# State space of a hybrid block: the row of steps and the chain of decays move into the convolution's stage, ScalarE makes the decays, and the sums over stretches keep the constant stationary

## The reference, cut to what matters

```python
def ssd_chunked(x, dt, A, B, C):
    b, L = x.shape[0], x.shape[1]
    nc = L // CHUNK
    G, K, P, N = N_SSM_GROUPS, HEADS_PER_GROUP, SSM_HEAD_DIM, D_STATE
    xdt = (x * dt[..., None]).reshape(b, nc, CHUNK, G, K, P)
    dA = (dt * A).reshape(b, nc, CHUNK, G, K).transpose(0, 1, 3, 4, 2)
    Bc = B.reshape(b, nc, CHUNK, G, N)
    Cc = C.reshape(b, nc, CHUNK, G, N)
    A_cum = jnp.cumsum(dA, axis=-1)
    Lmat = segsum_exp(dA)
    CB = jnp.einsum("bclgn,bcsgn->bcgls", Cc, Bc)
    y_diag = jnp.einsum("bcgls,bcgkls,bcsgkp->bclgkp", CB, Lmat, xdt)
    decay_states = jnp.exp(A_cum[..., -1:] - A_cum)
    states = jnp.einsum("bclgn,bcgkl,bclgkp->bcgkpn", Bc, decay_states, xdt)
    chunk_decay = jnp.exp(A_cum[..., -1])
    ...   # prev: the states of all chunks before, h = chunk_decay * h + states
    prev = jnp.moveaxis(prev, 0, 1)
    y_off = jnp.einsum("bclgn,bcgkpn,bcgkl->bclgkp", Cc, prev, jnp.exp(A_cum))
    return (y_diag + y_off).reshape(b, L, G, K, P)

def ssd_branch(z, xbc, dt_raw, conv_w, conv_b, dt_bias, a_log, d_skip, norm_w):
    b, L = z.shape[0], z.shape[1]
    xbc = jax.nn.silu(causal_depthwise_conv(xbc, conv_w, conv_b))
    ...
    xh = xs.astype(jnp.float32).reshape(b, L, N_SSM_GROUPS, HEADS_PER_GROUP, SSM_HEAD_DIM)
    dt = jax.nn.softplus(dt_raw.astype(jnp.float32) + dt_bias.astype(jnp.float32))
    dt = dt.reshape(b, L, N_SSM_GROUPS, HEADS_PER_GROUP)
    A = -jnp.exp(a_log.astype(jnp.float32)).reshape(N_SSM_GROUPS, HEADS_PER_GROUP)
    y = ssd_chunked(xh, dt, A, Bs.astype(jnp.float32), Cs.astype(jnp.float32))
    y = y + d_skip.astype(jnp.float32).reshape(N_SSM_GROUPS, HEADS_PER_GROUP)[..., None] * xh
    ...
```

## Time and profile before

| | us |
|---|---|
| median of 3 timed runs | 3831.87 (3828.68 to 3834.31) |
| the profiled execution | 3840.37, its span 3839.1 |
| mean granted clock of TensorE | 0.974 |
| PE busy | 3601.2, 94% of the span |
| DVE busy | 2043.1, 53% |
| ACT busy | 1398.2, 36% |
| POOL busy | 388.6, 10% |
| convolution's stage | from 660 to 820 |
| chain of steps | from 820 to 834 |
| state space | from 834 to 941 |

### The profile page before, as it was taken

How to read it: one execution, slowest core, us unless ns; L and a number is a source line. 1 busy time by engine, 2 the same in 40 slices (tenths; PEclk the granted TensorE clock), 3 DMA queues, 4 the chain that set the end, 5 groups by cost and what they waited for, 6 DMA issues and landing times. The chain is left out here.

```text
span 3839.1 us, 44288 instructions
## 1 busy us (share of the span) xinstructions
PE 3601.2 (94%) x17148; PEld 2924.7 (76%) x17148; DVE 2043.1 (53%) x3283; ACT 1398.2 (36%) x2423; POOL 388.6 (10%) x362
## 2 busy tenths in 40 slices
PE   8999999988998999989999989998999998989999
PEld 7877877876776887767887778877776777767777
DVE  4546465769536424741344466666466475562256
ACT  2224343321523223536223353354343232343244
POOL 1000000036001100013010100000000123121100
PEclk9999999989999999999999999999999999999999
DMA  6445311210223323520322232254201220132355
GB/s 235 176 173 179 116 39 61 88 40 28 84 92 115 124 94 127 171 71 6 105 81 75 93 99 94 94 174 142 82 23 48 72 77 12 39 111 88 93 178 162
DMA packets 106126, 380.16 MB, mean 99 GB/s; under 512 B 11760, under 2 KB 14592, under 8 KB 105792
## 3 DMA queue, kind: packets, MB, share of 16 engines
q1 hardware_dynamic: 100944, 364.86, 29.1%
q0 software_dynamic: 2896, 10.38, 0.9%
q10 hardware_dynamic: 2080, 2.10, 0.2%
HBM read 375.19 MB, written 2.10 MB: 98 GB/s over the span
## 5 line engine op out<-in xcount | busy, mean ns | idle before, releaser
L396 DVE TENSOR_TENSOR w_low<-ring,w_high 128x1024 fp32r<-128x1024 f32 (+1 forms) x637 | 811.9, 1275 | 1019.9 <-ACT w_high L384 1012.5
L420 PE MATMUL bank<-x_low,w_high 128*128 128x512 f32 (+1 forms) x2560 | 1000.2, 394 | 58.3 <-DVE w_low L396 15.8
L384 ACT ACTIVATE w_high<-ring 128x1024 fp32r<-128x1024 f32 (+1 forms) x637 | 670.6, 1053 | 897.1 <-PE bank L420 375.7
L420 PE MATMUL bank<-x_high,w_low 128*128 128x512 f32 (+1 forms) x2560 | 989.2, 390 | 0.0
L420 PE MATMUL bank<-x_high,w_high 128*128 128x512 f32 (+1 forms) x2560 | 636.0, 387 | 0.0
L420 PEld LDWEIGHTS bank<-x_low,w_high 128*128 128x128 f32 x2560 | 495.4, 194 | 162.1 <-issue 23.8
L420 PEld LDWEIGHTS bank<-x_high,w_low 128*128 128x128 f32 x2560 | 496.0, 194 | 97.0 <-issue 1.4
L420 PEld LDWEIGHTS bank<-x_high,w_high 128*128 128x128 f32 x2560 | 467.1, 192 | 99.2 <-issue 1.9
L482 PE MATMUL bank<-w_low,x_high 128*128 128x512 f32 (+3 forms) x416 | 156.9, 377 | 1.4 <-ACT z_z L1665 1.3
L484 PE MATMUL bank<-w_high,x_high 128*128 128x512 f32 (+3 forms) x416 | 155.7, 374 | 0.0
L483 PE MATMUL bank<-w_high,x_low 128*128 128x512 f32 (+3 forms) x416 | 155.5, 374 | 0.0
(11 more groups left out here) (624 smaller groups left out, 5738.2 us busy)
## 6 DMA issues: line engine op xcount, KB each, us to landing
ring<-in_W SPq DMA_DIRECT2D x688, 512.0 KB, 3.5
f_hid<-in_xT ACTq DMA_DIRECT2D x2, 1024.0 KB, 11.6
X<-in_x POOLq DMA_DIRECT2D x1, 2048.0 KB, 11.8
out<-X SPq DMA_DIRECT2D x4, 512.0 KB, 3.8
const<-in_consts POOLq DMA_DIRECT2D x1, 1389.0 KB, 6.1
f_norm<-in_ln_g POOLq DMA_DIRECT2D x2, 512.0 KB, 8.9
f_norm<-in_ln_b POOLq DMA_DIRECT2D x2, 512.0 KB, 10.6
ring<-in_W SPq DMA_DIRECT2D x2, 432.0 KB, 3.1
```

Of the source, the lines that this page charges most:

```text
L384: ac.activation(b.UH[i % NU][:, 0:src.shape[1]], src, ACT.Copy).then_inc(*b.split.act.up("high", i))
L396: dv.tensor_tensor(b.UL[i % NU][:, 0:n], src, b.UH[i % NU][:, 0:n].bitcast(F32), SUB).then_inc(*b.split.dve.up("low", i))
L420: i = pe.matmul(out, w[:, k, c], v, start=n == 0 and q == 0, stop=last and q == 3 * K - 1)
```

## The change

- dt1's unit comes before x1's in the list, and its matmuls, splits and additions before the convolution's tiles.
- The convolution's tiles run in the order 16 to 23, then 0 to 15 (`ORDER1`); the buffers go by position n instead of by m.
- The chain runs inside the convolution: ScalarE's part behind the copy of n=1, VectorE's behind n=3, PE's behind n=5, the exp into E3 behind the copy of n=7.
- LH is made by ScalarE, 8 activations (Copy with a pointer scale) of 128x128 per unit, two units ahead, instead of by POOL; it is now `incl` * DA.
- seg has the constant `after` as its stationary operand and LH as the moving one, 512 columns in one matmul, instead of LH stationary and `incl` moving, 128 columns in each of four.
- ScalarE no longer waits for the convolution's seal; LH, EE, CB and the softplus buffers lie apart from the convolution's buffers. PE waits for the last silu ahead of each bc.

```diff
@@ Mix1.__init__
+        self.LH = [a.take("s1_lh", 8, 128) for _ in range(2)]
+        sp = Area(b, a.at)
+        self.sp = [sp.take("s1_tmp", 4, 32) for _ in range(3)]
+        self.EE = [a.take("s1_ee", 8, 128) for _ in range(2)]
+        self.CB = [a.take("s1_cb", 128) for _ in range(2)]
         at = a.at
         self.cb = [a.take("c1_in", 516) for _ in range(3)]
...
@@ mix1_units
-    for m in range(24):
+    rows_units(b, s.gcv, "dt1", "w_in", [(ODT, 32)])
+    for m in ORDER1:
         b.unit(("x1", m), "w_in", down_rows(8), [(OX + 128 * m, 128)], lambda m=m: s.gcv.pe.at("x1", m))
-    rows_units(b, s.gcv, "dt1", "w_in", [(ODT, 32)])
...
+ORDER1 = list(range(16, 24)) + list(range(16))
+def tensor_steps(b, s):
     ...   # the three products of DA, out of tensor_ssd1
...
@@ tensor_conv1
+    tensor_rows(b, g, "dt1", b.x, lambda t: b.bank(("dt1", t), g.dve.at("dt", t)))
+    for n, m in enumerate(ORDER1):
...
+        turn(n - 1)
+        if n == 5:
+            tensor_steps(b, s)
+    turn(23)
...
@@ scalar_conv1
+    scalar_rows_ahead(b, "dt1")
+    for n, m in enumerate(ORDER1):
...
+        if n == 1:
+            ac.wait_ge(*g.dve.at("dt", 3))
+            scalar_softplus(b, s.gd.act, "dt", s.DT, s.sp[0])
+            ac.wait_ge(*b.arrived("a_log"))
+            ac.activation(s.al, s.al, ACT.Exp).then_inc(*s.gd.act.up("a"))
+        if n == 7:
+            ac.wait_ge(*s.gd.pe.at("e3"))
+            ac.activation(s.E3, b.bk["e3"][:, 0:384].rearrange("p (c q h) -> p c q h", c=4, q=3),
+                          ACT.Exp).then_inc(*s.gd.act.up("e3"))
...
+        if n >= 11:
+            ac.wait_ge(*g.pe.at("turned", ORDER1[n - 3]))
...
@@ vector_conv1 (its dt additions first)
+        turn(n - 1)
+        if n == 3:
+            vector_steps(b, s)
...
@@ tensor_ssd1
+            pe.wait_ge(*s.gcv.act.at("silu", 23))
             pe.matmul(bank.ap[:, 0:128], s.BT[:, q, sl], s.CT[:, q, sl], start=True,
                       stop=True).then_inc(*g.pe.up("bc", i))
-            pe.wait_ge(*g.pool.at("lh", i))
+            pe.wait_ge(*g.act.at("lh", i))
             for h in range(2):
...
-                for k in range(4):
-                    x = pe.matmul(bank.ap[:, k * 128:(k + 1) * 128], s.LH[i % 2][:, 4 * h + k, :], incl,
-                                  start=True, stop=True)
-                x.then_inc(*g.pe.up("seg", i, h))
+                pe.matmul(bank.ap, b.const("after"), s.LH[i % 2][:, 4 * h:4 * h + 4, :], start=True,
+                          stop=True).then_inc(*g.pe.up("seg", i, h))
...
@@ scalar_ssd1
+    def decays(i):
+        if i >= 16:
+            return
+        c, q = s.ssd[i]
+        if i >= 2:
+            ac.wait_ge(*g.pe.at("seg", i - 2, 1))
+        for k in range(8):
+            h = q * 8 + k
+            x = ac.activation(s.LH[i % 2][:, k, :], b.const("incl"), ACT.Copy, scale=s.DA[:, c, h:h + 1])
+            x.then_inc(*(f.up("lh", i) if k == 7 else f.up()))
+
+    for i in range(2):
+        decays(i)
     for i in range(16):
...
+        decays(i + 2)
...
@@ gpsimd_ssd1
-    gp.wait_ge(*g.dve.at("da"))
     gp.wait_ge(*g.act.at("e3"))
...
-        if i >= 2:
-            gp.wait_ge(*g.pe.at("seg", i - 2, 1))
-        gp.tensor_tensor(s.LH[i % 2], bc(b.const("after"), 1, 8), bc(s.DA[:, c, q * 8:q * 8 + 8], 2, 128),
-                         MUL).then_inc(*f.up("lh", i))
...
@@ scalar_program
     scalar_conv1(b, m1)
     b.seal("conv1", "act")
-    for w in b.sealed("conv1"):
-        ac.wait_ge(*w)
     scalar_ssd1(b, m1)
```

More of the change, by code:

```diff
@@ L1130, in __init__ @@
         a = Area(b, at)
[L1131 to L1135, removed]
         self.XD = [a.take("s1_xd", 512) for _ in range(3)]
@@ L1376, in scalar_att1 @@
             ac.activation(es, es, ACT.Exp).then_inc(*f.up("exp", i))
[L1382 to L1405, removed]
@@ L1408, in scalar_conv1 @@
[L1408 to L1421, removed]
@@ L1424, in vector_conv1 @@
[L1424 to L1440, removed]
-        dv.tensor_scalar(y, x[:, 0:512], b.col("conv_w", m), b.col("conv_b", m), MUL, ADD).then_inc(*f.up())
-        for j in range(1, 4):
-            dv.wait_ge(*f.now())
-            dv.scalar_tensor_tensor(y, x[:, j:j + 512], b.col("conv_w", 24 * j + m), y, MUL,
-                                    ADD).then_inc(*(f.up("conv", m) if j == 3 else f.up()))
[L1446 to L1453, removed]
@@ L1456, in gpsimd_conv1 @@
-def gpsimd_conv1(b, s):
-    for i in range(3):
-        b.nc.gpsimd.memset(s.cb[i][:, 0:3], 0.0).then_inc(*s.gcv.pool.up("zero", i))
-def tensor_ssd1(b, s):
+ORDER1 = list(range(16, 24)) + list(range(16))
+def tensor_steps(b, s):
     pe, g = b.nc.tensor, s.gd
-    incl, units, N = b.const("incl"), s.ssd, 16
     bank = b.bank("e3", g.act.at("e3"))
@@ new lines, in vector_steps, with vector_conv1, turn @@
+def vector_steps(b, s):
+    dv, g, f = b.nc.vector, s.gd, s.gd.dve
+    vector_softplus(b, f, g, "dt", s.DT, *s.sp)
+    dv.wait_ge(*f.now())
+    dv.wait_ge(*g.act.at("a"))
+    dv.scalar_tensor_tensor(s.DA, s.DT, -1.0, bc(s.al, 1, 4), MUL, MUL).then_inc(*f.up("da"))
+def vector_conv1(b, s):
+    dv, g, f = b.nc.vector, s.gcv, s.gcv.dve
+    vector_rows_ahead(b, "dt1")
+    dv.wait_ge(*b.arrived("dt_bias"))
+    for t in range(4):
+        dv.wait_ge(*g.pe.at("dt1", t))
+        dv.tensor_tensor(s.DT[:, t, :], b.bk["dt1", t][:, 0:32], s.dtb, ADD).then_inc(*f.up("dt", t))
+    def turn(n):
+        if n < 0 or ORDER1[n] >= 20:
+            return
+        m = ORDER1[n]
+        dst = s.BM[:, :, m - 16, :] if m >= 16 else s.XS[:, :, m * 128:(m + 1) * 128]
+        dv.wait_ge(*g.pe.at("turned", m))
+        dv.tensor_copy(dst, b.bk["xt1", m].rearrange("p (t c) -> p t c", t=4)).then_inc(*f.up("turned", m))
+    dv.wait_ge(*g.pool.at("zero", 2))
+    for n, m in enumerate(ORDER1):
+        vector_ahead(b, ("x1", m))
+        x, y = s.cb[n % 3], s.cy[n % 3]
+        dv.wait_ge(*g.act.at("copied", m))
+        if n >= 3:
+            dv.wait_ge(*g.act.at("silu", ORDER1[n - 3]))
+        dv.tensor_scalar(y, x[:, 0:512], b.col("conv_w", m), b.col("conv_b", m), MUL, ADD).then_inc(*f.up())
+        for j in range(1, 4):
+            dv.wait_ge(*f.now())
+            dv.scalar_tensor_tensor(y, x[:, j:j + 512], b.col("conv_w", 24 * j + m), y, MUL,
+                                    ADD).then_inc(*(f.up("conv", m) if j == 3 else f.up()))
+        turn(n - 1)
+        if n == 3:
+            vector_steps(b, s)
+    turn(23)
@@ L1476, in tensor_ssd1, with gpsimd_conv1 @@
+def gpsimd_conv1(b, s):
+    for i in range(3):
+        b.nc.gpsimd.memset(s.cb[i][:, 0:3], 0.0).then_inc(*s.gcv.pool.up("zero", i))
+def tensor_ssd1(b, s):
+    pe, g = b.nc.tensor, s.gd
+    units, N = s.ssd, 16
     for r in range(N + 4):
@@ L1544, in vector_ssd1 @@
     units, N = s.ssd, 16
[L1545 to L1548, removed]
     dv.wait_ge(*g.act.at("e3"))
```

35 lines of the change are left out of this document (28 added, 7 removed).

## The result

The changed kernel takes 3807.3 us (median of four runs, 3799.5 to 3813.3), the kernel before 3830.4 in the runs beside it: ratio 0.9937, 95% interval 0.9916 to 0.9958, so 24 us less, 16 to 32. A second comparison gave 0.9934 (0.9913 to 0.9954).

A forecast was written before the change was run, and what follows sets the result against it. TensorE was taken to bound the convolution, latency the chain, VectorE the state space. Terms 2.0 - 0.4 + 2.6 + 13.7 + 82.1 + 1.0 = 101.0 us against 120.8, so -19.8: median 3812.1 us, range 3806.5 to 3824.5.

The forecast's parts named there:

- B: State space rounds: VectorE's long instructions are not GpSimd's doing, rounds stay at 7.1 us; gain 5.9 us, chance 0.09.
- C: State space: ScalarE loads tables in every unit, 6.0 us per round instead of 5.6; gain 15 us, chance 0.04.
- D: Pipeline fill and state space: the clock stays at the half level, slower than before, say 3840 us; chance 0.05.
- A: State space: GpSimd's skip holds VectorE up elsewhere, +1.0 us in 12 rounds; gain 7.8 us, chance 0.12.
- step 7: State space rounds: VectorE 5.60 us and TensorE 5.62, level; y(0) to z1 82.1 us plus 1.0 for stalls.
- step 5: Convolution's tail, no longer covered by dt1: y(0) 13.7 us after the last tile's end, bounds 11.6 and 16.
- Steps 1 to 3: Up to the convolution's end: dt1 ahead of x1 +2.0 us, tile order -0.4, chain moved into the convolution +2.6.
- Step 6: seg in the state space: two matmuls of 512 columns replace eight of 128, 1.72 us instead of 2.12.

The follow-up runs named there:

- the GpSimd run: The changed kernel with the decays made by GpSimd again, in one instruction per unit; ratio 0.9985 to the kernel before.
- the run with eight matmuls: The changed kernel with seg in eight matmuls of 128 columns again, decays still by ScalarE; ratio 0.9932 to the kernel before.
- the second execution: The changed kernel run again with no edit; ratio 0.9934 to the kernel before.
- the move alone: The kernel before with only dt1 in front, BT and CT first and the chain in the convolution; decays by GpSimd, seg in eight matmuls; ratio 0.9983.

## Why the mechanism was right and the sum too small

The mechanisms held; the size did not. Most of my signs were there: the sum at 0.68 in ten of twelve rounds, TensorE's idle time in the rounds gone, no idle TensorE around tiles 4 to 7, L1394 inside the convolution without a wait, one table load behind the last silu, the rounds nearly level between VectorE (77.3 us) and TensorE (79.45). Three had other sizes: rounds of 5.45 us instead of 5.6 to 5.7, decays of 2.44 instead of 2.2, y(0) after 12.5 us instead of 14. B fell (the GpSimd run), C fell (one load, 3.3 us a unit), D fell (half clock only until 835.5). A came up in the first two rounds with yo, and in three of the run with eight matmuls, and cost nothing.

The sum was -19.8 and the stretch says -24.2 (z1's shift -24.0). What failed is the price of TensorE's round in step 7, and with it a smaller part of step 5. By the steps:

- *Steps 1 to 3, up to the last tile's end:* I had it move by 16.3 + 2.0 - 0.4 + 2.6 = 20.5; it moved from 803.67 to 824.78, 21.1. The half clock behind dt1 cost 2.5 (677 to 682), in the bounds of 0 to 5; L1394 cost 2.60. 0.6 too little. The chain under cover cost nothing, as I had it.
- *Step 5, the fill:* 13.7 forecast, 12.5 measured. The mis-sized part is the clock: I had the full level back 8.1 us behind the silu, in the middle of seg(1), counted from seg(0) on, though the last turn and bc(0) stand ahead of it (829.33). It was back at 835.5 (6.2 us behind the silu), with seg(1) just begun (835.56), so bc(1) took 0.42 instead of 0.7 and seg(1) 1.72 instead of 2.5. In the second execution it came back within seg(1), which took 1.99.
- *Step 7, the rounds, is the term that carried most of the miss:* 83.1 forecast, 79.45 measured. bc was taken at 0.39 from the earlier trace rows; in the changed kernel it is 0.22: 14 x 0.17 = 2.4. The 1.0 for stalls did not come up, though VectorE was only 2 us from full. These two are 3.4 of the 3.65.
- *Step 6:* seg's new form at 1.72 was right (1.73), so the sum is not touched, but the credit was wrong. The old form costs 1.78 in flow; my 2.12 held the standing time of a stalled round. The wide matmuls are worth 0.05 us a unit, and nearly all of the gain in the rounds is ScalarE's taking over of the decays.

0.6 - 1.2 - 3.65 = -4.2 us: this is the difference. What goes with the 0.39 can be read in the kernel before itself, in its last round with seg, where nothing waits behind bc or inside seg:

```profile
930.85 0.49 PEld L1510 LDWEIGHTS bank<-m_ct,m_bt 128*128 128x128 f32 x2 [0.36 <-DVE s_yt L1566]
931.15 0.39 PE L1510 MATMUL bank<-m_ct,m_bt 128*128 128x128 f32 x2
```

bc is 0.39 there too, and seg 1.86. What this round shares with the stalled ones is the wait in front: bc's weight loads had stood 0.36 us for VectorE's yo. All the 0.38 and 0.42 us rows of the move alone and of the GpSimd run that lie in rounds of 7.1 us have this wait (0.36 to 0.40), and no 0.22 us row of the changed kernel has it. The kernel before has 0.22 itself, at 846.41 and 867.32, where the loads did not stand so. So in the rounds of 7.1 us VectorE's lateness goes with longer instructions on TensorE, in bc and in seg, and I carried the price of bc over into rounds in which VectorE is not late. No run tests that wait alone.

The two pages of the Trainium skill. "ScalarE: Activation LUTs", section "What ACT_TABLE_LOAD costs", gave a drain on top of the load; at n=1 the rows are

```profile
691.60 1.28 ACT L1083 ACT_TABLE_LOAD   x1
692.89 0.31 ACT L1083 ACTIVATE s_tmp<-s_tmp 128x128 f32<-128x128 f32 x1
```

so the next activation starts 1.29 us after the load does, the one ahead had ended at 691.58, 0.02 before it, and TensorE is not late at n=1 or n=7: the measurement speaks against the page here. "SBUF — State Buffer", section "Who interferes with whom", held in each row: the sum (two SBUF inputs) ends behind GpSimd's instruction both in the GpSimd run (2.19) and in the eight-matmul run (1.34), and L1598 takes 1.15 beside L1639.

## What to carry to other kernels

Take what a TensorE step costs from rows where TensorE flows, and look for another row of the same form before a stalled one is used; look at the weight loads too, since a wait of theirs went with a longer step here and shows in no idle time of the matmuls. When an elementwise step on GpSimd with large inputs lies beside VectorE's, price the move to ScalarE by VectorE's lengthened instruction, not by the step itself. Look at the granted clock over every run of narrow matmuls: turned round, with 512 moving columns and a stationary of 128 of which 32 are used, they took a third of the time here, and gave another 12 us, half of what the whole change gave.

## What was not expected of the hardware

- The clock falls under a busy TensorE: with 96 matmuls of 32 columns back to back it fell to the half level 2.4 to 5.1 us after their start in all nine traces with dt1 in this form, in front of the convolution or behind it. As 24 matmuls of 512 columns the same products kept the full level, in all five runs with that form, with 32 and with 128 stationary columns. Narrow matmuls cost 0.11 us each before the fall and 0.21 after it.
- 24 fp32r matmuls with 32 stationary columns into 32 partitions took the expected 5.66 us but did not give the values of the 128-column form. The cause is open.
- An activation of 128x128 with a pointer scale runs at 0.30 us (8 in 2.44, 16 in 4.76 to 4.92), half an Exp of 128x512 (0.60) for a quarter of the elements.
